# Latent attention between two feed-forward layers: its heads in two groups, with projections and the output projection placed between the attention rounds

## The reference, cut to what matters

```python
cq, ckv, k_rope = split(h @ w_dqkv, [384, 640])            # 384 + 256 + 32 columns
q  = (rms_norm(cq, q_lora_norm)   @ w_uq ).reshape(16 heads, 64 + 32)
kv = (rms_norm(ckv, kv_lora_norm) @ w_ukv).reshape(16 heads, 64 + 64)
q_nope, k_nope = rms_norm(q_nope), rms_norm(k_nope)        # per head, over 64
q_rope = rope(rms_norm(q_rope))                            # per head, over 32
k_rope = rope(rms_norm(k_rope))                            # one for all heads
s = (q_nope @ k_nope^T + q_rope @ k_rope^T) * 96 ** -0.5   # causal
o = softmax(s) @ v
x = x + o @ w_o
```

## Time and profile before

| | |
|---|---|
| median of 3 runs | 1361.05 us (1359.34 to 1361.91) |
| the profiled execution, its own time | 1360.02 us |
| its span, first to last instruction | 1358.2 us |
| TensorE busy | 1295.7 us (95%) |
| weight loads of TensorE | 1106.1 us (81%) |
| VectorE busy | 920.8 us (68%) |
| ScalarE busy | 712.7 us (52%) |
| GpSimd busy | 43.3 us (3%) |
| mean granted TensorE clock | 0.986 |
| chain that ended last | PE 89%, DVE 5%, ACT 3% |

### The profile page before, as it was taken

One profiled execution on the slowest core, in us unless ns is written; L12 is line 12 of the kernel. 1 busy time (PEld: TensorE's weight loads), 2 busy tenths in 40 slices (PEclk: granted clock), 3 DMA queues, 4 the chain that ended last, 5 costly groups with the idle time before them and its releaser, 6 DMA issues.

```text
span 1358.2 us, 17587 instructions
## 1 busy us (share of the span) xinstructions
PE 1295.7 (95%) x7034; PEld 1106.1 (81%) x7034; DVE 920.8 (68%) x1270; ACT 712.7 (52%) x1074; POOL 43.3 (3%) x80
## 2 busy tenths in 40 slices
PE   6999999999999878999999999999998998999997
PEld 5998678888888767888888877888888996788886
DVE  4967565676666676666667756666666895776665
ACT  5865344554445654555445544544446664544443
POOL 0000000000000400000000000000000000000000
PEclk9999999999999889999999999999999998999999
DMA  6453235455555311455555543555554321455551
GB/s 241 156 186 124 94 110 200 155 187 187 186 186 169 143 62 47 144 213 186 187 186 187 198 152 126 184 186 189 187 188 166 109 79 62 155 187 186 202 186 62
DMA packets 30785, 215.17 MB, mean 158 GB/s; under 512 B 3552, under 2 KB 3808, under 8 KB 5488
## 3 DMA queue, kind: packets, MB, share of 16 engines
q1 hardware_dynamic: 30704, 214.05, 44.0%
HBM read 212.99 MB, written 1.05 MB: 158 GB/s over the span
## 4 chain that ended last, share of the span: by engine, by line
PE 89%; DVE 5%; ACT 3%; issue 1%; POOL 0%; DMA 0%; SPq 0%; POOLq 0%; ACTq 0%; DVEq 0%
PE pb L428 24%; PE pb L399 15%; PE pb L401 14%; PE pb L400 14%; PE pb L430 12%; PE pb L913 3%; PE pb L405 2%; DVE wlo L1432 2%; ACT arena L980 1%; DVE arena L1436 1%; ACT both L980 1%; DVE both L1445 1%; PE pb L754 1%; ACT whi L976 1%; PE pb L531 0%
## 5 line engine op out<-in xcount | busy, mean ns | idle before, releaser
L1432 DVE TENSOR_TENSOR wlo<-raw,whi 128x2048 fp32r<-128x2048 f32 (+2 forms) x201 | 453.3, 2272 | 233.8 <-ACT whi L976 233.7
L428 PE MATMUL pb<-both,whi 128*128 128x512 f32 x1408 | 498.4, 398 | 6.5 <-DVE both L1445 4.3
L976 ACT ACTIVATE whi<-raw 128x2048 fp32r<-128x2048 f32 (+2 forms) x201 | 379.3, 1893 | 39.9 <-PE pb L401 35.6
L430 PE MATMUL pb<-both,wlo 128*128 128x256 f32 x1408 | 394.9, 280 | 0.0
L428 PEld LDWEIGHTS pb<-both,whi 128*128 128x128 f32 x1408 | 264.4, 188 | 73.3 <-issue 5.1
L399 PE MATMUL pb<-whi,both 128*128 128x512 f32 (+1 forms) x754 | 298.0, 395 | 11.2 <-DVE both L1445 5.3
L401 PE MATMUL pb<-whi,both 128*128 128x512 f32 (+1 forms) x754 | 294.1, 390 | 0.0
L400 PE MATMUL pb<-wlo,both 128*128 128x512 f32 (+1 forms) x754 | 293.5, 389 | 0.0
L430 PEld LDWEIGHTS pb<-both,wlo 128*128 128x128 f32 x1408 | 265.8, 189 | 1.4
L980 ACT ACTIVATE arena<-pb 128x256 f32<-128x256 f32 (+1 forms) x248 | 103.5, 426 | 252.1 <-PE pb L430 171.8
L399 PEld LDWEIGHTS pb<-whi,both 128*128 128x128 f32 x754 | 142.7, 189 | 44.7 <-issue 8.6
(11 more groups left out here) (117 smaller groups left out, 913.6 us busy)
## 6 DMA issues: line engine op xcount, KB each, us to landing
raw<-d_ws SPq DMA_DIRECT2D x196, 1024.0 KB, 4.9
raw<-d_ws SPq DMA_DIRECT2D x3, 768.0 KB, 4.3
arena<-d_c SPq DMA_DIRECT2D x1, 1060.0 KB, 4.8
xt<-d_x SPq DMA_DIRECT2D x2, 512.0 KB, 4.2
arena<-d_rows SPq DMA_DIRECT2D x2, 512.0 KB, 5.2
out<-arena SPq DMA_DIRECT2D x2, 512.0 KB, 2.6
raw<-d_ws SPq DMA_DIRECT2D x1, 640.0 KB, 3.8
c<-d_c SPq DMA_DIRECT2D x1, 385.0 KB, 5.4
```

What stands on the lines that cost most here:

```text
L428: e.matmul(b[:, :], wh[:, k, fs], both[:, k, :], start=k == 0, stop=k == 7, skip_group_check=True)
L430: m = e.matmul(b[:, 256:512], wl[:, k, fs], ahi[:, k, :], start=False, stop=k == 7, skip_group_check=True)
L976: e.activation(whi[:, n % NH, 0:width(n)], raw[:, n % NR, 0:width(n)], ACT.Copy).then_inc(*sig("act.hi", f"hi{n}"))
L1432: e.tensor_tensor(wlo[:, n % NH, 0:width(n)], raw[:, n % NR, 0:width(n)], f32(whi[:, n % NH, 0:width(n)]), ALU.subtract).then_inc(*sig("dv ...
```

## The change

- The chunks of `w_uq` and `w_ukv` alternate in `PLAN`: rope part, queries 0 to 7, keys and values 0 to 7, queries 8 to 15, keys and values 8 to 15.
- The norms of `cq` and `ckv` are not multiplied in before the transposes. They enter as the scale of the squares, of the copy of the values, and of the product that scales the heads (`scale_heads`, a `scalar_tensor_tensor`). The 160-column product is cut in two with the transposes of `cq` between the halves (`part`).
- Before the rounds only the rope part, queries 0 to 7, keys and values 0 to 7 and queries 8 to 15 are projected. Keys and values 8 to 15 are projected in rounds 0 to 3 (`project` in the loop).
- `turn_p` and `mix` follow one and two rounds behind `attend`, in place of two and three. The sums of `mix` are kept in one bank for four heads and both tiles, in place of eight heads and one tile.
- From round 6 on the output projection runs inside the loop (`rows_part`, `MLA_OUT_AT`), with the conversions of the next chunks of weights in rounds 6, 9 and 12. From round 5 on the ring has banks 0 to 3 alone, since banks 4 to 7 hold the sums.
- The roots of units 6 to 9 (queries and keys of heads 8 to 15) are taken on GpSimd with its power operation; rope is done for eight heads at a time, into two tiles of its own.

```diff
@@ -66,8 +66,9 @@
     plan += moving("w_in", 0, 1024)
     plan += rows("w_out", 8)[4:] + rows("w_out", 8)[:4] + ffn("0")
     plan += moving("w_dqkv", 0, 512) + [("w_dqkv", 0, 8, 512, 160)]
-    plan += [("w_uq", 0, 3, 512 * j, 512) for j in range(3)]
-    plan += [("w_ukv", 0, 2, 1024 * j, 1024) for j in range(2)]
+    plan += [("w_uq", 0, 3, 0, 512)]
+    for j in range(2):
+        plan += [("w_uq", 0, 3, 512 * j + 512, 512), ("w_ukv", 0, 2, 1024 * j, 1024)]
...
+MLA_UNITS = [("R", 0, 0), ("R", 0, 1), ("Q", 0, 0), ("Q", 0, 1), ("K", 0, 0), ("K", 0, 1), ("Q", 1, 0), ("Q", 1, 1),
+             ("K", 1, 0), ("K", 1, 1)]
+MLA_HEADS_AT = {1: (2,), 2: (3,), 4: (4, 5), 5: (6,), 6: (7,)}
+MLA_OUT_AT = {6: (0, (0,)), 7: (0, (1, 2)), 8: (0, (3,)), 9: (1, (0,)), 10: (1, (1, 2)), 11: (1, (3,)), 12: (2, (0, 1)),
+              13: (2, (2, 3))}
 MLA_ROUNDS = [x for h in range(0, 16, 4) for x in ((0, h, 4), (1, h, 2), (1, h + 2, 2))]
-KV_SLOTS = (8, 9, 10, 11, 0)
+MLA_SLOTS = {"R": (8, 9, 10), "Q": (8, 9, 10), "K": (11, 0), "V": (11, 0)}
+def mla_chunk(kind, g):
+    return CHUNK["w_ukv", g] if kind in "KV" else CHUNK["w_uq", 1 + g if kind == "Q" else 0]
+def att_slots(j):
+    return 1 + 2 * j, 2 + 2 * j
+def mla_scales(i):
+    return (16 * i, 16) if i < 2 else (32 + 8 * (i - 2), 8)
...
+            def rows_part(key, n, bs, slots, ready, parts, first):
+                wh, wl = weights(n)
+                for i in parts:
+                    t, c = i // 2, i % 2
+                    for k, slot in enumerate(slots):
+                        e.wait_ge(*at(ready[k]))
+                        m = mm3(bs[i][:, :], ahi[:, slot, 128 * t:128 * t + 128], alo[:, slot, 128 * t:128 * t + 128],
+                                wh[:, k, half(c)], wl[:, k, half(c)], first and k == 0, False)
+                if 3 in parts:
+                    m.then_inc(*sig(key, f"done{n}"))
...
-                moving(key, n0 + 2, bs, 160, 0, "dqm1")
-                turn_slots(key, "cqT", lambda t, j: T.cq[:, t, 128 * j:128 * j + 128], 3, "cqn1")
+                part(n0 + 2, bs, 160, range(4))
+                turn_slots(key, "cqT", lambda t, j: T.cq[:, t, 128 * j:128 * j + 128], 3, "dq0.1.gone")
+                part(n0 + 2, bs, 160, range(4, 8)).then_inc(*sig(key, "dqm1", f"done{n0 + 2}"))
...
+                project("R", 0, 0)
+                project("R", 0, 1)
+                turn_slots(key, "kvT", lambda t, j: T.cq[:, t, 384 + 128 * j:512 + 128 * j], 2, "dq1.1.gone")
+                for kind in "QKV":
+                    project(kind, 0, 0)
+                    project(kind, 0, 1)
+                project("Q", 1, 0)
+                project("Q", 1, 1)
                 turn_heads(0)
                 turn_heads(1)
-                for i in range(15):
+                for i in range(14):
+                    if i == 5:
+                        ring.over = (0, 1, 2, 3)
                     if i < 12:
                         attend(i)
-                    if i % 3 and i < 10:
-                        turn_heads(2 + 2 * (i // 3) + (i % 3 - 1))
-                    if 2 <= i < 14:
-                        turn_p(i - 2)
-                    if i >= 3:
-                        mix(i - 3)
-                def turn(j):
-                    turn_slots(key, f"at{j}", lambda t, i: T.o[:, t, 128 * (2 * j + i):128 * (2 * j + i) + 128], 2,
-                               f"att{j // 2}.1")
-                bs = open_out(2)
-                ring.over = (0, 1, 2, 3)
-                turn(0)
-                for j in range(4):
-                    if j < 3:
-                        turn(j + 1)
-                    s0 = 8 + (2 * j) % 4
-                    rows_out(key, 2, CHUNK["w_o", j], bs, (s0, s0 + 1), (f"alo{j}.0", f"alo{j}.1"), j == 0, j == 3)
+                    if i >= 2:
+                        mix(i - 2)
+                    if i < 4:
+                        project("KKVV"[i], 1, i % 2)
+                    for hp in MLA_HEADS_AT.get(i, ()):
+                        turn_heads(hp)
+                    if i == 6:
+                        bs = open_out(2)
+                    if i in MLA_OUT_AT:
+                        j, parts = MLA_OUT_AT[i]
+                        rows_part(key, CHUNK["w_o", j], bs, att_slots(j), (f"alo{j}.0", f"alo{j}.1"), parts, j == 0)
+                    if i in (5, 8, 11):
+                        turn((i - 5) // 3)
+                    if 1 <= i < 13:
+                        turn_p(i - 1)
+                turn(3)
+                rows_out(key, 2, CHUNK["w_o", 3], bs, att_slots(3), ("alo3.0", "alo3.1"), False, True)
...
+                def square_heads(i):
+                    kind, g, t = MLA_UNITS[i]
+                    e.wait_ge(*at(f"pjm.{kind}{g}.{t}"))
+                    e.wait_ge(*at("mla.rkv" if kind == "K" else "mla.rq"))
+                    if i >= 2:
+                        e.wait_ge(*at(f"red{i - 2}"))
+                    else:
+                        own()
+                    a = (10 if kind == "K" else 8) + t
+                    run(key, f"hsq{i}", T.sqb[i % 2], bank(f"pj.{kind}{g}.{t}")[:, :], ACT.Square, scale=st[:, a:a + 1])
...
                 turn_heads(0)
                 turn_heads(1)
-                for i in range(15):
+                for i in range(14):
                     if i < 12:
                         attend(i)
-                    if i % 3 and i < 10:
-                        turn_heads(2 + 2 * (i // 3) + (i % 3 - 1))
-                    if 2 <= i < 14:
-                        turn_p(i - 2)
...
+                    if i == 0:
+                        hi(mla_chunk("K", 1) + 2)
+                    if i < 2:
+                        square_heads(8 + i)
+                    if i in (2, 3):
+                        values(1, i - 2)
+                    for hp in MLA_HEADS_AT.get(i, ()):
+                        turn_heads(hp)
+                    if i in (6, 9, 12):
+                        hi(CHUNK["w_o", (i - 6) // 3] + 2)
+                    if i in (5, 8, 11):
+                        turn((i - 5) // 3)
+                    if 1 <= i < 13:
+                        turn_p(i - 1)
+                turn(3)
+                hi(CHUNK["w_o", 3] + 2)
...
+                def scale_heads(i):
+                    kind, g, t = MLA_UNITS[i]
+                    a, n = mla_scales(i)
+                    heads = (T.kf if kind == "K" else T.qt)[:, t, 8 * g:8 * g + n, :]
+                    dst = heads[:, :, 64:96] if kind == "R" else heads[:, :, 0:64]
+                    s = (10 if kind == "K" else 8) + t
                     e.wait_ge(*at(f"root{i}"))
...
+                    if i < 6:
+                        recip(key, [], T.stats[:, a:a + n])
+                        own()
+                    stt(key, [f"pj.{kind}{g}.{t}.gone"] + {1: ["qrope"], 5: ["heads0"], 9: ["heads1"]}.get(i, []), dst,
+                        cut(bank(f"pj.{kind}{g}.{t}")[:, :], n), st[:, s:s + 1],
+                        bc(T.stats[:, a:a + n], [P, n, 512 // n], 2), ALU.mult, ALU.mult)
...
+                reduce_heads(6)
+                reduce_heads(7)
+                scale_heads(6)
                 turn_heads(0)
                 turn_heads(1)
-                for i in range(15):
+                for i in range(14):
                     if i < 12:
                         attend(i)
-                    if i % 3 and i < 10:
-                        turn_heads(2 + 2 * (i // 3) + (i % 3 - 1))
-                    if 2 <= i < 14:
-                        turn_p(i - 2)
-                    if i >= 3:
-                        mix(i - 3)
...
+                    if i >= 2:
+                        mix(i - 2)
+                    if i == 0:
+                        lo(mla_chunk("K", 1) + 2)
+                    if i < 2:
+                        reduce_heads(8 + i)
+                        scale_heads(7 + i)
+                    if i == 2:
+                        scale_heads(9)
+                    for hp in MLA_HEADS_AT.get(i, ()):
+                        turn_heads(hp)
+                    if i in (6, 9, 12):
+                        lo(CHUNK["w_o", (i - 6) // 3] + 2)
+                    if i in (5, 8, 11):
+                        turn((i - 5) // 3)
+                    if 1 <= i < 13:
+                        turn_p(i - 1)
+                turn(3)
+                lo(CHUNK["w_o", 3] + 2)
...
+                def rope_heads(g):
+                    heads = T.qt[:, :, 8 * g:8 * g + 8, :]
+                    own()
+                    rope(key, heads[:, :, :, 64:80], heads[:, :, :, 80:96],
+                         [bc(x, [P, 2, 8, 16], 2) for x in T.tabs[0:4]], T.ra4, T.rb4, f"rope{g}")
+                def root(i):
+                    a, n = mla_scales(i)
+                    e.wait_ge(*at(f"red{i}"))
+                    rstd(key, f"root{i}", T.stats[:, a:a + n], 64)
                 e.wait_ge(*at("qrope"))
```

(8 more changed lines are left out.)

233 lines of the change are left out of this document (104 added, 129 removed).

## The result

The changed kernel takes 1372.24 us, the median of 4 runs (1371.52 to 1374.19), against 1360.19 (1357.08 to 1361.91) for the kernel before beside it: a ratio of 1.0093, 95% interval 1.0071 to 1.0116. It is slower, as forecast (1370.5, range 1358 to 1377), by 12.05 us instead of 9.5.

The account below looks back on a forecast made before the run. No engine was full; handing over from TensorE to VectorE to ScalarE and back set the pace. Mix 0 at 493.1 + 54.1 work + 14.7 waits = 561.9, +9.7 us on 1360.02 or the median: forecast 1370.5, range 1358 to 1377.

Parts of the forecast that it names:

- Ahead of the rounds: Before round 0: rope block gains 5.4 us, not kept as VectorE and ScalarE lead; round 0 starts at 476.2, 9.3 earlier.
- Rounds 0 and 1: Second tile of keys 8 to 15: TensorE idles 5.1 us for bank 4, behind VectorE's scaling; mix 0 at 493.1.
- Round 7: Ahead of mix 5: TensorE waits 3.95 us for the copy of P 5 behind `lo`, to 520.9; another 0.75 in the round.
- The wait ahead of mix 8: Round 10: TensorE waits 2.1 us, since `hi` stands ahead of the copy of P 8 in round 9.
- The end of the layer: Where the next stage's transposes begin: 561.9, against 552.37 before, +9.7 us.
- the work from mix 0 on: TensorE's scores, mixes, transposes and products from mix 0 to the layer's end: 54.1 us, with 14.7 of waits besides.
- the third rival: Rounds 7 and 10: output projection products at the lower clock, 2.5 us each, +5 us, to 1376; chance 0.13.
- the forecast of +9.7: End of the attention layer: 9.7 us later than before, 561.9 against 552.37.
- The rule on the clock: TensorE: a 2.87 us gap behind busy work leaves the clock up; lower clock counted in rounds 0 and 1 alone.
- Rival 1: In the rounds, work fills TensorE's gaps: layer ends at 540.2, 12.2 us earlier, total 1349; chance 0.15.
- The wait for bank 4: Rounds 0 and 1: second tile of keys 8 to 15 waits 5.1 us until unit 7's scaling frees the bank.

Follow-up runs that it names:

- k1: The changed kernel with TensorE's waits ahead of mixes 5 and 8 filled by 30 and 13 transposes of the unit matrix: 1368.96 us, ratio 1.0064 to before.
- l1: f2 with TensorE's waits ahead of scores 0 and mix 0 filled by 38 and 16 transposes: 1359.54 us, ratio 0.9989 to before.
- f2: f1 with round 0's conversion split to rounds 2 and 3, unit 7's scaling behind mask 0, roots of units 6 and 7 on ScalarE: 1360.94 us, ratio 1.0012.
- h1: The kernel before with only the norms at the heads and the 160-column product split around the transposes: 1355.46 us, ratio 0.9965.
- f1: The changed kernel with ScalarE's later weight conversions behind the copy of P (rounds 6, 9, 12), VectorE's in rounds 7, 10, 12: 1366.63 us, ratio 1.0056.

## Why the prediction was right, and where it was off

- **Ahead of the rounds: right.** The rope block starts 16.95 us into the layer, 3.4 earlier, with products every 0.23 us. That VectorE and ScalarE would not keep it is right too: scores 0 at 472.94, on the clock of the earlier trace rows (3.12 more, so that both layers start together) 476.06, forecast 476.2. The power on eight columns takes 1.64 us, forecast 1.65; the rope of eight heads 6.41, forecast 7.2, and no one waits for it.
- **Rounds 0 and 1: right in place and cause, 0.8 us too small.** 5.94 against 5.1 us, ahead of the last six products of the keys, put down to VectorE's scaling; mix 0 at 493.5 on that clock, forecast 493.1. The prediction's words that TensorE has by then "one projection pair more" done are the wrong way round: a pair is still owed. Its sum has that right, with the 12 products behind mix 0.
- **Round 7: right.** 3.60 us against 3.95 ahead of mix 5, for the copy behind `lo`, at 521.1 against 520.95. The wait ahead of mix 8 is 1.64 against 2.1. From mix 0 on the waits of the timeline add up to 11.65 us; I had 14.7.
- **The end of the layer: off.** Forecast 561.9, measured 567.0 on that clock. The step that failed is the work from mix 0 on, 54.1 us, priced at the upper clock throughout. It took 61.8 (73.46 less the 11.65 of waits). 5.1 of the 7.7 us more are half of 10.2 us at the lower clock behind mixes 5 and 8; the other 2.6 are, within 0.5, what I had booked as waits and the lines show as work. I had the mechanism as the third rival, at +5 and 0.13: it deserved the greater chance, since it needs only that waits of 4 and 2 us be followed by what had followed the 4.15 us ahead of round 0 before. k1 shows it as a cause: with the waits filled the clock stays at 1.0 from there on, and the layer is 4.4 us shorter, of the 4.9 that the forecast of +9.7 missed.
- **The rule on the clock.** The granted clock fell behind or within each of the four long waits of the changed kernel, and stayed up in k1 and l1 where they were filled with work. The Trainium skill, TensorE: Matmul & The Clock Gate, What's actually happening, has it that the slow clock is the default state and activity releases it; by that rule the sum would have been the third rival's, and the traces agree with it. Which wait brings the clock down isn't told by its length alone: none did behind 2.87 us before and behind 2.43 in f2 and l1, while 2.82 at that same place in h1, 2.43 in f1 and 1.64 in the changed kernel were followed by the lower level. The prediction's own reading, that a gap of 2.87 us behind a busy stretch leaves the clock up, doesn't hold as a rule.
- **The total was nearer than the layer.** 1370.5 against 1372.24: in the profiled execution the layer's excess was partly hidden by a start 3.1 us earlier, and executions differ in how much they spend at the lower clock. That the total came within 2 us is luck in this part: the layer was missed by 4.9.
- **Rival 1** (the work fills the gaps) fell with every wait in its place. It is what the design could give, and f2 and l1 show why it doesn't: with the conversions moved as in f2 the layer is at 124.0, and 120.9 with the clock held, not 110.5. VectorE's and ScalarE's hand-over ahead of scores 0 (4.9 us) and in the rounds stays.

**Where the expected gain went:** the earlier rope block, worth 5.1 us in h1, was still worth 3.9 at scores 0. The wait for bank 4 ate that, and from mix 0 on the conversions between the rounds made further waits, which were followed by the lower clock. f2 takes back 13.3 us of waits and clock together, k1 4.4 of the clock alone. The 6.5 us between f2 and h1 stay unexplained.
